# A two-block transformer kernel on one core: the column of marks grows from 40 to 48 words, and the tiles behind it move up by 32 bytes

## The reference, cut to what matters

```python
def swiglu(h, w_gate_up, w_down):
    gt, up = jnp.split(h @ w_gate_up, 2, axis=-1)
    return (jax.nn.silu(gt) * up) @ w_down
...
    h = rmsnorm(x, norm_g)
    proj = h @ w_in
...
    merged = g_a * (y_a @ w_out_a) + g_b * (y_b @ w_out_b) + g_c * (y_c @ w_out_c)
    return x + merged @ w_o
```

## Time and profile before

| | us |
|---|---|
| median of 3 runs (lowest, highest) | 1442.72 (1441.86, 1445.33) |
| the profiled execution, its time on the device | 1449.57 |
| the same, from its first instruction to its last (its span) | 1447.7 |
| TensorE busy | 1430.0 |
| VectorE busy | 1041.2 |
| ScalarE busy | 850.4 |
| GpSimd busy | 89.7 |

### The profile page before, as it was taken

How to read it: one execution, slowest core, us unless ns; L and a number is a source line. 1 busy time by engine, 2 the same in 40 slices (tenths; PEclk the granted TensorE clock), 3 DMA queues, 4 the chain that set the end, 5 groups by cost and what they waited for, 6 DMA issues and landing times.

```text
span 1447.7 us, 30461 instructions
## 1 busy us (share of the span) xinstructions
PE 1430.0 (99%) x11772; PEld 1352.4 (93%) x11772; DVE 1041.2 (72%) x1782; ACT 850.4 (59%) x1482; POOL 89.7 (6%) x144
## 2 busy tenths in 40 slices
PE   8999999999999999999999999999999999999999
PEld 5888999999989999999998989899999898989999
DVE  2878898888676678755675857886676685787664
ACT  4566666555556756445466776565566676665553
POOL 0111011110000000000001000220000100021000
PEclk9999999999999999999999999999999999999999
DMA  9966699996664365666564545336666355534663
GB/s 364 339 212 217 239 332 336 344 345 230 202 235 157 118 213 188 222 181 187 187 213 124 173 159 161 117 119 196 196 193 211 115 170 162 160 108 132 190 201 121
DMA packets 81122, 291.93 MB, mean 202 GB/s; under 512 B 9185, under 2 KB 10465, under 8 KB 80882
## 3 DMA queue, kind: packets, MB, share of 16 engines
q1 hardware_dynamic: 68274, 244.31, 51.7%
q0 software_dynamic: 11728, 42.64, 8.7%
q10 hardware_dynamic: 1008, 3.41, 0.6%
HBM read 289.27 MB, written 1.05 MB: 201 GB/s over the span
## 4 chain that ended last, share of the span: by engine, by line
PE 90%; DVE 5%; ACT 2%; issue 1%; DMA 1%; SPq 0%; DVEq 0%; ACTq 0%
PE G L537 23%; PE G L538 22%; PE G L539 22%; PE G L596 2%; PE G L598 2%; PE G L597 2%; DVE wlo L1766 2%; PE Tp L990 1%; ACT whi L1227 1%; PE O L1162 1%; PE Tp L932 1%; PE S L1128 1%; PE S L1057 1%; DVE aw L1774 1%; PE Tp L716 1%
## 5 line engine op out<-in xcount | busy, mean ns | idle before, releaser
L1766 DVE TENSOR_TENSOR wlo<-raw,whi 128x1024 fp32r<-128x1024 f32 x442 | 541.5, 1228 | 251.9 <-ACT whi L1227 250.4
L1227 ACT ACTIVATE whi<-raw 128x1024 fp32r<-128x1024 f32 x442 | 466.5, 1058 | 214.5 <-PE G L539 160.8
L537 PE MATMUL G<-h,whi 128*128 128x256 f32 x2064 | 584.5, 283 | 0.3 <-DVE wlo L1766 0.2
L538 PE MATMUL G<-h,whi 128*128 128x256 f32 x2064 | 573.3, 278 | 0.0
L539 PE MATMUL G<-h,wlo 128*128 128x256 f32 x2064 | 573.3, 278 | 0.0
L537 PEld LDWEIGHTS G<-h,whi 128*128 128x128 f32 x2064 | 388.2, 188 | 9.5 <-issue 8.4
L539 PEld LDWEIGHTS G<-h,wlo 128*128 128x128 f32 x2064 | 389.3, 189 | 0.0
L538 PEld LDWEIGHTS G<-h,whi 128*128 128x128 f32 x2064 | 388.2, 188 | 0.7 <-issue 0.5
L1774 DVE CUSTOM_DVE_ANT_0 aw<-aw,cs,cols 128x1024 f32<-128x1024 f32 x80 | 101.5, 1279 | 0.0
L537 PE MATMUL G<-ah,whi 128*128 128x256 f32 x352 | 98.2, 279 | 0.0
L538 PE MATMUL G<-ah,whi 128*128 128x256 f32 x352 | 98.2, 279 | 0.0
(11 more groups left out here) (438 smaller groups left out, 2325.8 us busy)
## 6 DMA issues: line engine op xcount, KB each, us to landing
raw<-in_w SPq DMA_DIRECT2D x444, 512.0 KB, 3.9
aw<-in_ada POOLq DMA_DIRECT2D x80, 512.0 KB, 5.1
adaw<-in_ada SPq DMA_DIRECT2D x8, 1024.0 KB, 15.3
sn<-in_uq ACTq DMA_DIRECT2D x2, 768.0 KB, 4.6
x<-in_x SPq DMA_DIRECT2D x1, 1024.0 KB, 5.2
pt<-in_ukv ACTq DMA_DIRECT2D x2, 512.0 KB, 5.8
out<-x SPq DMA_DIRECT2D x4, 256.0 KB, 2.3
dec<-in_dec ACTq DMA_DIRECT2D x1, 512.0 KB, 8.0
```

The source lines that it names most:

```text
L537: pe.matmul(o, wh, mv[:, 0:T], start=(k == 0), stop=False)
L538: pe.matmul(o, wh, mv[:, T:2 * T], start=False, stop=False)
L1227: act.activation(whi[:, s, :], raw[:, s, :], ACT.Copy).then_inc(w_hi, 1)
L1766: dve.tensor_tensor(wlo[:, s, :], raw[:, s, :], whi[:, s, :], ALU.subtract).then_inc(w_lo, 1)
```

## The change

One number: the column of marks is allocated with 48 words for 40.

```diff
-        mark = sb("mark", [P, 40])
+        mark = sb("mark", [P, 48])
```

## The result

| | before | after |
|---|---|---|
| median of 9 runs, us (lowest, highest) | 1445.33 (1441.86, 1453.23) | 1457.27 (1456.76, 1459.17) |
| the profiled execution, us | 1449.57 | 1457.32 |
| its span | 1447.7 | 1455.5 |
| TensorE busy | 1430.0 | 1438.1 |

The changed kernel is slower by 0.83% (ratio 1.0083, 95% interval 1.0066 to 1.0101), 12 us between the medians. The forecast was 1454 us, +11.4 us, in a range of 1438 to 1465 us. The column of before holds the three runs from which the forecast started (median 1442.72) and six more, which pushed the median up.

What follows compares the result with a forecast made beforehand. TensorE's matmul cadence was taken as the bound: 10.2 us on fast and 1.2 us on slow matmuls of moved tiles, all else 0, put +11.4 us on 1442.72, giving 1454 us, range 1438 to 1465 us.

Steps and rivals of the forecast that it cites:

- The bound: TensorE, busy 1430.0 of 1447.7 us: time is number of matmuls times distance between starts, plus about 18 us idle.
- the sum: 2928 matmuls on moved tiles: 1896 x (118.9 - 113.5) plus 1032 x (118.9 - 117.7) ns, +11.4 us; other parts 0.
- the sign: In the changed profile, `ah` between 284 and 342 us should have a median duration of 282 to 285 ns for 277.
- The part that I read from `h` and its two cadences: On `h`, 113.4 or 117.8 ns: moving-tile and weight reads meet in one of two relative positions, so addresses can matter.
- one 64-byte piece more: A tile moved by 32 bytes reads into one more 64-byte piece per matmul, costing up to 120.0 ns.
- The 258-wide matmuls: 48 matmuls from 349.77 to 355.57 us, 120.8 ns each, giving 120.0 ns as upper bound for 256 columns.
- The term: Cadence of a 256-column matmul on a moved tile: 118.9 ns, the middle between 117.7 and 120.0.
- a cost per matmul is the same in every execution: Step from profiled span to median: the same 11.4 us go on the median of 1442.72, giving 1454 us.
- Nothing happens: Rival: reads go in units of 16 or 32 bytes and addresses don't matter; 1443 us, chance 0.25.
- the rule of 16-byte lines: SBUF has full bandwidth within 16-byte lines; 1024 bytes cover 64 lines from either start, so the sum would be 0.
- Faster: Rival: slow stages on `yr`, second half of `ah`, start of `yh` turn fast, 4.3 us less; 1438 us, chance 0.14.
- Slower, and `h` with it: Rival: in hybrid layers' last stage 1152 `h` matmuls turn slow, 4.8 us more; 1462 us, chance 0.16 including a worse place.

Runs made afterwards that it cites:

- 64 behind: Kernel before with marks of 72 words, so the moved tiles start 64 bytes modulo 256 behind the weights; 1464.35 us, ratio 1.0146.
- 128 behind: Kernel before with marks of 88 words, so the moved tiles start 128 bytes modulo 256 behind the weights; 1464.00 us, ratio 1.0118.
- 192 behind: The kernel before, whose activation tiles start 192 bytes modulo 256 behind the weights; 1443.3 to 1445.3 us, ratio 1.
- the change undone: Changed kernel without the four 8-word gaps behind `cmask`, so all tiles behind it are at their old addresses; 1444.24 us, ratio 1.0017 to the kernel before.
- 224 behind: The changed kernel, marks of 48 words for 40, moved tiles starting 224 bytes modulo 256 behind the weights; 1457.27 us, ratio 1.0083.

## Why the prediction was right, and where it was lucky

**The bound.** Right. TensorE's busy time grew by 8.1 us and the span by 7.8, with the waits within 0.2 us of those before. (The waits for a rounded block are 5.4 us before and not 3.0 in all, since line 674 has one of 2.4 us, in both kernels; the sum doesn't rest on it.) VectorE, ScalarE and the transfers, taken as 0, cost 0. `ah` from 284 us went from 340 to 355.3 ns a triple, inside the forecast 353 to 360, and `h` from 174 to 283 us stayed at 340. The median duration of `ah`, 280 or 281 ns, is below the 282 to 285 that I had named as the sign.

**The mechanism.** The part that I read from `h` and its two cadences held in what it says of addresses: where the one tile lies against the other counts. The weights moved by 64 bytes show it. That two reads meet is my explanation of it, and no run looks into that. The other part, one 64-byte piece more, was wrong. I had taken the 258-wide matmuls as its evidence. Marks of 56 words add no piece and cost more (119.9 ns); everything moved by 32 bytes adds a piece and leaves both cadences where they were. The 258-wide matmuls go by the distance too. With marks of 72 and of 88 words their tile starts on a multiple of 64 bytes as before, so that they reach into the same number of pieces; the same 48 of them, from the first to the matmul behind the last:

```profile
354.18 0.28 PE L659 MATMUL G<-yr,whi 128*128 128x258 f32 x1
...
359.90 0.28 PE L537 MATMUL G<-h,whi 128*128 128x256 f32 x1
```

```profile
354.48 0.28 PE L659 MATMUL G<-yr,whi 128*128 128x258 f32 x1
...
360.34 0.28 PE L537 MATMUL G<-h,whi 128*128 128x256 f32 x1
```

5.72 us / 48 = 119.2 ns at 64 behind, 5.86 / 48 = 122.1 ns at 128 behind, for 120.8 at 192. So the earlier trace rows were no measure of a piece. Why two columns more cost 7 ns at 192 behind stays open.

**The term.** 118.9 ns was the middle between 117.7 and 120.0; 118.4 was measured. The two ends served as bounds by luck: the upper one came from the piece, and the nine distances tried other than 192 lie between 116.7 and 120.0 ns.

**The counts.** This is where the sum and the medians agree by luck. With 118.4 ns the sum is 1896 x 4.9 + 1032 x 0.7 = 10.0 us. Taken over all matmuls, from each start to the next, the two profiled executions differ so: those on the five moved tiles cost 9.0 us more (`yh` 3.4, `ah` 2.8, `mh` 1.8, `oh` 0.8, `yr` 0.1), `h` in the second feed-forward got the fast cadence in the trace of after and gave 3.8 us back, `h` everywhere else cost 3.2 us more, and all other matmuls 0.6 us less. That is the 7.8 us of the spans. The medians differ by 12 us; a median run of before would then have fewer stages in the slow cadence than its profiled one, which no trace of a median run shows. There is luck in the base too: the forecast put 11.4 us on 1442.72, the median of three runs, and 1457.27 is 14.6 above that. The step that failed is "a cost per matmul is the same in every execution". It isn't, at 192 behind. Against an execution in which nearly all are fast (the one of the change undone, 1442.59 us) the sum is 2928 x 4.9 = 14.3 us, and the two profiled executions differ by 14.7: 12.5 on the moved tiles, 2.7 on `h`, 0.5 less elsewhere. So even there the moved tiles paid less than the sum, and `h`, which I had taken as unchanged, paid the rest.

**The rivals.** "Nothing happens" fell, and with it the rule of 16-byte lines, which the prediction takes from the Trainium skill (SBUF — State Buffer, in the specifications and under Door 1), as an account of this case. A shift by a whole number of 16-byte lines changes the cadence: 113.5 to 118.4 ns on `ah`. "Faster" fell: stretches that were slow became slower (117.7 to 118.4 ns), not fast. "Slower, and `h` with it" happened at 64 behind, and at 224 behind in part. Views of `h` in the changed kernel, each right behind 24 matmuls on `yh`, from 976.3 us (the first such place of the stage) and from 1001.4 us:

```profile
L537 PE MATMUL G<-h,whi x16: 281/281/282, 976.3 to 981.6; 128*128 128x256 f32 x16
...
L537 PE MATMUL G<-h,whi x15: 276/276/286, 1001.4 to 1006.2; 128*128 128x256 f32 x15
```

In the first, `h` keeps the slow cadence for all of its 48 matmuls (5.3 us / 15 = 353 ns a triple). In the second, 4.8 us / 14 = 343 ns: it is back at the fast one after a few matmuls, as I had said against that rival, and so it is in the rest of the stage. Both layers do this, which costs about 1 us of the 4.8 that the rival had.

## What to carry to other kernels

Where TensorE runs fp32r matmuls back to back and is the bound, take the distance between starts before anything else, stage by stage, and compare it with columns over clock (here 106.7 ns). If it differs between stages of the same shape, or moves when a tile is shifted, treat the addresses of the moving tile and of the weights modulo 256 as a parameter of the kernel, to be measured at each distance: nothing in this table could have been interpolated. A gap above columns over clock doesn't tell by itself, since the best distance here has 6.7 ns of it too. And compare several runs of each version: one profiled execution can be 7 us off another of the same addresses. And any edit to the list of tiles, even of one that nobody reads, moves all tiles behind it; fix the places of the hot tiles so that such an edit can't.

## What the runs showed of the hardware

- Back-to-back fp32r matmuls of 128x128 by 256 columns at the granted 2.4 GHz have a cadence that depends on how far the moving operand starts from the stationary one modulo 256 bytes: 113.4 or 117.7 ns at 192 behind, 116.7 to 120.0 ns at the nine other distances tried, with two values each at 128 (118.7 and 120.0) and 160 (117.4 and 118.6). It isn't smooth at 16 bytes.
- At 192 behind two cadences are steady. A stage keeps one until a start comes late, or until matmuls on a tile at another distance come between, and different executions of the same addresses differ. Of the twelve profiled executions in which `h` lies 192 behind the weights, its stage from 600 us is fast in eight and slow in four. The length of the late start ahead of it doesn't tell which: 160 and 170 ns have each led into both.
- The runs of the kernel before spread from 1441.86 to 1453.23 us, those of the changed kernel, whose moved tiles have one cadence, over 2.4 us. That the draws make most of the wider spread is shown for two executions only: 1449.57 and 1442.59 us differ by 7.0, and the three stages that were slow in the one and fast in the other (`h` and `ah` of the second feed-forward, `yr`) come to 7.7.
- VectorE's 426 and 416 ns for one operation on two tiles stayed within 1 ns when both tiles changed their place modulo 64.
- Open: what the matmuls wait for, why 192 alone reaches 113.4 ns, what decides between the two cadences of a distance, and why moving everything by 32 bytes makes the slow one more frequent. That the weights' distance and not another tile's is meant was shown with one shift of the weights, by 64 bytes, and with the five tiles moved to the same distance from the other side, which gave the same two cadences. The cadence of each distance is from one profiled execution.
